# Which engine computes the weight residuals of the expert stage: thirteen units from GpSimd to VectorE

## The reference

```python
def hierarchical_moe(h, ...):        # 512 tokens x 1024
    # top-1 group of 4, then top-2 experts of the 4 in that group
    ...
    a = jnp.einsum('td,edf->tef', ht, w_gate)      # 16 experts, 1024 -> 256
    u = jnp.einsum('td,edf->tef', ht, w_up)
    hid = jax.nn.silu(a) * u * combine[..., None]
    out = jnp.einsum('tef,efd->td', hid, w_down)   # 256 -> 1024
```

## Time and profile before

| | us |
|---|---|
| median of 3 runs | 1744.12 (1742.73 to 1746.04) |
| the profiled execution's own time | 1744.98 |
| its span | 1743.2 |
| PE busy | 1655.1 (95%) |
| DVE busy | 875.6 (50%) |
| ACT busy | 775.9 (45%) |
| POOL busy | 125.0 (7%) |

### The profile page before, as it was taken

The page is one execution under the profiler, slowest core; times in us unless marked ns, Lnnn a source line. Parts: engine busy times, 40 slices in busy tenths (PEclk is TensorE's granted clock), DMA queues, the critical chain, the costliest instruction groups (busy, mean ns, idle before and its releaser), DMA issues.

```text
span 1743.2 us, 20038 instructions
## 1 busy us (share of the span) xinstructions
PE 1655.1 (95%) x7715; PEld 1308.7 (75%) x7715; DVE 875.6 (50%) x1010; ACT 775.9 (45%) x901; POOL 125.0 (7%) x87
## 2 busy tenths in 40 slices
PE   6999999999998889859999999999999999999998
PEld 5777777887876777647688888876788688888886
DVE  6434434444577777747642342421355665565464
ACT  5553454223467666727443343351223543443333
POOL 2101101000222223210010000000000000000000
PEclk8999999999999999979999999999999999999999
DMA  7456553223599999931421211131323133333322
GB/s 226 133 188 222 193 179 123 77 82 125 168 342 346 355 330 323 327 139 49 143 68 49 73 57 64 62 110 49 121 87 105 51 97 105 89 96 98 95 79 67
DMA packets 183202, 247.82 MB, mean 142 GB/s; under 512 B 10236, under 2 KB 151000, under 8 KB 179808
## 3 DMA queue, kind: packets, MB, share of 16 engines
q1 hardware_dynamic: 178911, 232.21, 40.4%
q0 software_dynamic: 4224, 14.72, 2.1%
HBM read 233.23 MB, written 13.67 MB: 142 GB/s over the span
## 4 chain that ended last, share of the span: by engine, by line
PE 78%; DVE 9%; DMA 5%; ACT 4%; issue 2%; SPq 1%; POOL 0%; ACTq 0%; DVEq 0%; POOLq 0%
PE psum L409 20%; PE psum L410 19%; PE psum L411 19%; DMA raw_more<-in_w_up 4%; DVE w_lo_more L1699 3%; PE psum L2466 2%; ACT w_hi_more L1694 1%; PE psum L709 1%; DVE w_lo L1699 1%; DVE pre L488 1%; PE psum L792 1%; PE psum L1203 1%; PE psum L1437 1%; PE psum L1204 1%; PE psum L1205 1%
## 5 line engine op out<-in xcount | busy, mean ns | idle before, releaser
L409 PE MATMUL psum<-h_hi,w_hi 128*128 128x512 f32 x1160 | 466.0, 402 | 7.7 <-DVE w_lo L386 3.2
L411 PE MATMUL psum<-h_hi,w_lo 128*128 128x512 f32 x1160 | 453.5, 391 | 0.0
L410 PE MATMUL psum<-h_lo,w_hi 128*128 128x512 f32 x1160 | 453.4, 391 | 0.0
L386 DVE TENSOR_TENSOR w_lo<-raw,w_hi 128x2048 fp32r<-128x2048 f32 (+2 forms) x99 | 223.7, 2259 | 228.4 <-ACT w_hi L382 228.4
L409 PEld LDWEIGHTS psum<-h_hi,w_hi 128*128 128x128 f32 x1160 | 218.4, 188 | 69.4 <-issue 18.4
L411 PEld LDWEIGHTS psum<-h_hi,w_lo 128*128 128x128 f32 x1160 | 218.6, 188 | 46.9
L410 PEld LDWEIGHTS psum<-h_lo,w_hi 128*128 128x128 f32 x1160 | 218.8, 189 | 46.4 <-issue 3.6
L382 ACT ACTIVATE w_hi<-raw 128x2048 fp32r<-128x2048 f32 (+2 forms) x100 | 187.9, 1879 | 75.3 <-PE psum L411 70.0
L1699 DVE TENSOR_TENSOR w_lo_more<-raw_more,w_hi_more 128x2048 fp32r<-128x2048 f32 x41 | 115.0, 2804 | 50.0 <-ACT w_hi_more L1694 50.0
L439 ACT ACTIVATE sq<-x 128x512 f32<-128x512 f32 x56 | 35.4, 632 | 161.0 <-DVE x L1316 105.2
L1694 ACT ACTIVATE w_hi<-raw 128x2048 fp32r<-128x2048 f32 x42 | 80.4, 1914 | 35.7 <-DMA raw<-in_w_up 16.6
(11 more groups left out here) (380 smaller groups left out, 2595.4 us busy)
## 6 DMA issues: line engine op xcount, KB each, us to landing
raw<-in_w_up SPq DMA_DIRECT2D x72, 512.0 KB, 6.5
wm_raw<-in_w_mod SPq DMA_DIRECT2D x24, 1024.0 KB, 5.9
raw<-in_w_in SPq DMA_DIRECT2D x18, 1024.0 KB
raw<-in_w_in SPq DMA_DIRECT2D x33, 512.0 KB
raw<-in_w_gate SPq DMA_DIRECT2D x28, 512.0 KB, 5.1
raw_more<-in_w_down SPq DMA_DIRECT2D x28, 512.0 KB, 6.2
raw<-in_w_down SPq DMA_DIRECT2D x28, 512.0 KB, 5.9
raw_more<-in_w_gate SPq DMA_DIRECT2D x27, 512.0 KB, 5.0
```

The source lines that it names most:

```text
L386: dve.tensor_tensor(w_lo[j][:, 0:tiles, :], raw[j][:, 0:tiles, :], w_hi[j][:, 0:tiles, :].bitcast(F32), ALU.subtract).then_inc(G["lo_ready ...
L409: pe.matmul(to, w_hi[j][:, tile, :], hi_k, start=(k == 0), stop=False)
L410: pe.matmul(to, w_hi[j][:, tile, :], lo_k, start=False, stop=False)
L411: return pe.matmul(to, w_lo[j][:, tile, :], hi_k, start=False, stop=last)
```

## The change

`POOL_UNITS` and `DVE_UNITS` go, with the two semaphores e_dlo and e_plo; one semaphore e_wlo counts all units in order. VectorE subtracts every unit, in order of use. GpSimd's stream keeps its DMAs alone. Loads, ScalarE and TensorE have the order they had.

```diff
         def wait_unit_lo(eng, u):
-            if u in POOL_UNITS:
-                eng.wait_ge(E["e_plo"], POOL_UNITS.index(u) + 1)
-            else:
-                eng.wait_ge(E["e_dlo"], DVE_UNITS.index(u) + 1)
+            eng.wait_ge(E["e_wlo"], u + 1)
...
             for n in range(STEPS):
                 s, e = n // PER_GROUP, n % PER_GROUP
-                if unit_down(n) in POOL_UNITS:
-                    unit_lo(pool, unit_down(n))
                 if e == 0 and s and s + 2 < SLOTS:
                     load_tokens(s + 2)
...
         def unit_lo(eng, u):
+            if u >= UNITS:
+                return
             b = u % 4
             eng.wait_ge(E["e_whi"], u + 1)
             eng.tensor_tensor(u_lo[b][:, :, :], raw_of(u)[:, :, :], u_hi[b][:, :, :].bitcast(F32), ALU.subtract)\
-               .then_inc(E["e_plo" if u in POOL_UNITS else "e_dlo"], 1)
+               .then_inc(E["e_wlo"], 1)
...
-                dve_lo(3 * n + 4)
-                dve_lo(3 * n + 5)
+                unit_lo(dve, 3 * n + 4)
+                unit_lo(dve, 3 * n + 5)
```

More of the change, by code:

```diff
@@ L1388, in build @@
         E = semaphores("e_wr", "e_matched", "e_chain", "e_shift", "e_exp", "e_routed", "e_scat", "e_gathered",
-                       "e_hg0", "e_hg1", "e_in0", "e_in1", "e_in2", "e_in3", "e_whi", "e_dlo", "e_plo", "e_used",
+                       "e_hg0", "e_hg1", "e_in0", "e_in1", "e_in2", "e_in3", "e_whi", "e_wlo", "e_used",
                        "e_turned", "e_hi", "e_lo", "e_silu", "e_hid", "e_ycopy", "e_ystore")
@@ L1574, in unit_down @@
             return min(3 * n + 4, UNITS - 1)
-        POOL_UNITS = [unit_down(n) for n in range(1, STEPS - 1, 2)]
-        DVE_UNITS = [u for u in range(UNITS) if u not in POOL_UNITS]
         def wait_unit_lo(eng, u):
-            if u in POOL_UNITS:
-                eng.wait_ge(E["e_plo"], POOL_UNITS.index(u) + 1)
-            else:
-                eng.wait_ge(E["e_dlo"], DVE_UNITS.index(u) + 1)
+            eng.wait_ge(E["e_wlo"], u + 1)
         def tokens_of(s):
@@ L1825, in moe_vector @@
         def moe_vector(dve):
-            def dve_lo(u):
-                if u in DVE_UNITS:
-                    unit_lo(dve, u)
             def tokens_lo(s):
@@ L1837, in moe_vector @@
             dve.tensor_copy(comb_s[:, 0, :], psum[:, HT_BANK, 0:PER_GROUP]).then_inc(E["e_routed"], 1)
-            dve_lo(1)
-            dve_lo(2)
-            dve_lo(3)
+            unit_lo(dve, 1)
+            unit_lo(dve, 2)
+            unit_lo(dve, 3)
             for n in range(STEPS):
@@ L1856, in moe_vector @@
                     tokens_lo(s + 1)
-                dve_lo(3 * n + 6)
+                unit_lo(dve, 3 * n + 6)
             split_lo(dve, G_PG, G_PG % 2)
```

## The result

| | before, us | changed, us |
|---|---|---|
| median of the runs beside one another | 1745.08 (1742.73 to 1752.32, 4 runs) | 1726.13 (1721.61 to 1729.18, 4 runs) |
| profiled execution, span | 1744.98, 1743.2 | 1724.20, 1722.4 |
| PE, DVE, POOL busy | 1655.1, 875.6, 125.0 | 1651.5, 884.6, 64.3 |

The ratio is 0.9882, with a 95% interval of 0.9844 to 0.9921: 19 us faster, where 14.5 were forecast, inside the range of 1722 to 1739.

What follows compares the result with a forecast made beforehand. PE and DMA engines were both near full, a chain of waits through g_lo taking the rest; 11.5 us from five slots, 1.0 and 2.0 from the end make 14.5, so about 1729.6 us, range 1722 to 1739.

Steps and rivals of the forecast that it cites:

- The stop of VectorE: Expert stage: GpSimd's subtraction excludes DVE's while it runs; 21.3 us of excess over the stage.
- DVE's additional work of 29.6 us: Expert stage: DVE takes GpSimd's 13 subtractions at 2.28 us each, hidden by DVE's idle time.
- The first sum: Expert stage: PE's 12 waits for g_lo before down, 18.7 us, of which about 16 us could go.
- The second sum: Expert stage: DMA engines' idle time, 17.5 us at most; a slot has 37.2 us of transfer time in 40.4.
- The last slot: Expert stage, 689.82 to 726.96 us: already 37.14 us long, at most about 1.3 us to gain, 1.0 taken.
- the last step: Expert stage, down to step 25 at 739.56: of its 3.86 us wait, 2.0 us go.
- The token loads: GpSimd's queue: slot 4's load comes some 20 us sooner; bounds 1.6 us gained or lost in each of four slots.
- the choice: Expert stage: between 16 and 17.5 us, DMA share rises from 0.92 to 0.975, so a slot takes 38.1 us.
- Outside the stage: Rest of the kernel: nothing is touched, the same time behind the stage as before.
- A: Expert stage: transfers take most of the gain back; 4 to 8 us gained, median about 1738 us; chance 0.18.
- B: Expert stage: nearly all PE idle time goes and the clock stays up; 18 to 22 us gained, 1724 us; chance 0.11.
- C: Expert stage: g_lo waits for two DVE subtractions in a row; 14.5 us slower, 1759 us; chance 0.04.

Runs made afterwards that it cites:

- run 3: Changed kernel plus 13 GpSimd subtractions on tiles nobody uses, which stop VectorE: 1743.96 us, ratio 0.9994 to the kernel before.
- run 7: Kernel before, GpSimd keeping its 13 units, with g_lo ahead of the residual of unit 3n + 5 on VectorE: 1743.52 us, ratio 0.9991.
- run 4: Changed kernel, but SP's queue and TensorE learn of unit 3n + 4's residual in odd steps two GpSimd memsets later: 1742.41 us, ratio 0.9993.
- run 5: Changed kernel with the two-memset late release in odd steps seen by SP's loads alone, not TensorE: 1741.32 us, ratio 0.9973.
- run 11: Changed kernel plus GpSimd's unused subtractions, with g_lo ahead of the residual of unit 3n + 5 on VectorE: 1732.72 us, ratio 0.9914.
- run 2: Changed kernel with the token loads held back to where they stood before: 1724.41 us, ratio 0.9876.
- experiment 1: Changed kernel again with no edit, on the chip of the next runs: 1723.65 us, ratio 0.9897 to the kernel before.
- run 6: Changed kernel with the two-memset late release in odd steps seen by TensorE's down alone, not SP's loads: 1728.63 us, ratio 0.9914.

## Why the prediction was right, and where it was off

*The stop of VectorE* was read rightly: 2.0 us of excess for 2.15 us of overlap, gone with GpSimd's subtraction; run 3 brings it back with unrelated tiles, as an exclusion does and a wait on data would not. DVE's additional work of 29.6 us was free, as worked out: in step 13 the new subtraction ends at 605.7, and DVE then idles 1.05 us before it starts the next.

*The first sum* (16 us of PE's waits for g_lo) had about the right size and the wrong cause: it took the waits for what the lateness of g_lo costs. Run 7 takes g_lo from behind the stretched subtraction and gains 2 us at equal clock, since in the kernel before the loads were late as well, and that alone costs nearly as much (runs 4 and 5). Whether g_lo's lateness costs more where the loads are otherwise on time is open (run 3 against run 11). The stop and the late release lie side by side in the same odd steps and do not add: by the medians 20 us for the one alone, 16 to 19 us for the other alone, 19 us for both; in the stages of the traces 13, 21 and 22.5 us. The change takes both away at once. So the agreement of the first sum with the gain was luck, and the forecast held by the second, which counts the idle time of the transfers whatever causes it.

*The second sum* is the term that was mis-sized. I took the transfer time of a slot, 37.2 us, as fixed, and so 17.5 us as the ceiling. The stage gained 22.5 us. A slot now takes 36.5 us at a share of 0.99, 36.1 us of transfer time for the same bytes: the share of busy time turned out to be no rate, and per unit of share the rate rose from 334 / 0.92 = 363 to 371 / 0.99 = 375 GB/s. That is 1.1 us a slot. The share reached 0.99 where I took 0.975, another 0.5 us. Over the five slots from step 0 to step 20 the forecast was 11.5 us; they took 672.20 - 487.97 = 184.2 us rather than 202.1, 17.9 us less. The last slot gave 2.1 us (1.0 forecast), the last step 2.5 (2.0). Seen from PE, the sum had no term for the clock: 5.0 of the 22.5 us are matmuls that ran at a higher granted clock.

*The token loads* moved by 20 us as read from the order, and are worth nothing (run 2). I had counted on a small gain inside the choice: it has no place in the sum.

*Outside the stage* "nothing is touched" was right of the work and not of the time: the stage ended 24.7 us sooner, the kernel 20.8 us, with the clock low in places where it had been full. The kernel's 19 us lie nearer to the forecast than the stage's 22.5 for this reason, which the forecast did not know.

*The rivals.* A (transfers take it back) did not come: ACT waits for the gate and up weights about as long as before, no longer. The Trainium skill (DMA: Bandwidth & Descriptors, Specifications) puts HBM at about 358 GB/s for one core, as half of what a stack gives. The stage now runs at 372 GB/s over 229 us, on the one core that runs here, so the measurement stands above the page's figure, and the ceiling that I drew from it was none. B came half true: PE is at 97%, the stage gained 22.5 us and the clock in it rose from 0.98 to 0.99, but the kernel gained 19. C (VectorE as the bound) did not come: DVE waits for ACT's w_hi in 46 of its subtractions, 35.1 us in all in the stage (the waits of the changed kernel above).

## What to carry to other kernels

Where two engines may exclude one another, look for a group whose mean is longer on some tiles than on others for the same shape, and lay the intervals of both engines over each other; the engine that looks idle may be the one that is stopping the busy one. In a ring of few buffers that is nearly full, what matters of a step is when it frees its buffer: 13 buffers freed 1.9 us late cost 14 us here, although TensorE was told of their residuals on time. And a wait in the profile is the place where lateness shows, not what it costs: the 18.7 us of waits for g_lo were worth about 2 us by themselves (run 7), and two causes in the same steps were each worth most of the gain. Where executions differ by their clock, medians of a dozen are not enough: set the traces of the stage beside them before a difference between two edits is called a cause.

## What the runs showed of the hardware

Run and run of one kernel differ by the granted clock. The eight runs of experiment 1 range from a span of 1719.4 us at a mean granted clock of 0.989 to 1735.4 us at 0.978; the runs of the kernel before beside them from 1736.0 us at 0.987 to 1753.8 us at 0.976. Both are about 1.5 us for each 0.001 of clock. At a clock of 0.987 the changed kernel has a span of 1720.7 us and the kernel before, in three executions, 1736.0 to 1739.3; by the lines through all executions, at 0.985, they are 15.7 us apart. So of the 19 us some 3 may be that the changed kernel drew the full clock more often. In the kernel before the low windows in the stage stood where PE had just idled: 0.86 and 0.79 from 615 and 620 us, around a wait of 2.31 us, and 0.66 from 680, behind one of 1.89 us. The changed stage has 0.99; its 2.09 us of idle time at 526 us had such a window (0.71 from 525), its 2.78 us at step 0 had none. Behind the stage the drops fell on other places from run to run, and what sets them off there stays open.

A GpSimd memset of 128 x 1024 (0.95 us), which reads nothing, leaves VectorE alone: with 26 of them in the stage VectorE's subtractions stayed at 2.289 us (runs 4 to 6), where 13 reading subtractions stretched them by 23.3 us. The Trainium skill (SBUF — State Buffer, Who interferes with whom) says the same: only GpSimd instructions that read SBUF contend with a two-input VectorE instruction.
